# Conditioning sums moved from TensorE to GpSimd, norms by blocks of tokens, and rotary angles made earlier, in a two-part transformer kernel

## The chip, the cores and the metric

The kernel runs on one core of one Trainium2 chip. Times are device microseconds of that core for one launch. In the texts PE is TensorE, DVE is VectorE, ACT is ScalarE, POOL is GpSimd and SP is SyncE, which only issues DMAs here. The first run of numbers below is the median of three runs; the rows are of one profiled execution.

## The reference

256 tokens of 1024 features pass through two parts. The first has two layers. Each makes six vectors of 1024 (shift, scale and gate for the mixer, and again for the feed-forward) from one conditioning vector:

```
cond = silu(c)
for l in range(2):
    mod = cond @ w_ada[l] + b_ada[l]                  # 1024 x 6144
    sh1, sc1, g1, sh2, sc2, g2 = split(mod, 6)
    h = rms_norm(x, g_norm_mix[l]) * (1 + sc1) + sh1
    z = h @ w_in[l]                                   # 1024 x 2884
    mix = concat(dsa_mixer(z), hgrn2_mixer(z), gmlp_mixer(z)) @ w_out[l]
    x = x + g1 * mix
    h = rms_norm(x, g_norm_ffn[l]) * (1 + sc2) + sh2
    y = swiglu(h) if l == 0 else moe_swiglu(h)        # 8 experts, top 2
    x = x + g2 * y
x = rms_norm(x, g_final)
```

The second part (a forgetting attention, two feed-forwards with a short convolution, and a sparse attention) has no conditioning. It has a rotary embedding of its own with other angles (`positions_2`), needed for the tokens and for 15 compressed keys. All arithmetic is fp32.

## The kernel before

**Weights.** All large weights pass through one ring. SP loads slots of 1 MB (128 partitions x 2048 values) into `raw`, six places deep, in a fixed order of names: ada00, in0, out0, ada01, ffn0, ada10, in1, out1, ada11, the experts, then the second part. ACT copies a slot to `w_hi` (L792, rounded to the short matmul type, four places), DVE subtracts to make `w_lo` (L1631, in the place of `raw`), and PE multiplies three times per tile (`three`, L1127 to L1129: high by high, high by low, low by high). `w_used` counts slots that PE is done with; SP's load of slot n waits for slot n−6. An ada stage is one of four: `ada{l}0` makes shift, scale and gate ahead of the mixer, `ada{l}1` those ahead of the feed-forward, each in 12 slots and six groups of 512 columns.

**An ada stage.** DVE and ACT spread the conditioning vector over 128 columns, as high and low part (L973, L1739), in the place of the activations' columns `xT`. PE multiplies it with the slots, so that each of the 128 rows of the result is the same. DVE adds each group into `arena[:, 0:3*D]`, where POOL's queue had loaded the bias (L723), spread over all partitions. `mod[:, 0]` is the shift, `mod[:, 1]` the scale, `mod[:, 2]` the gate. The stage waits for the gate's last use (`mod_free`), and the columns `xT` of the layer before it are done with.

**A norm.** `x_ready` is signalled by DVE after X is written. ACT squares X in two blocks of 128 tokens (L869) with a sum, DVE and ACT make the reciprocal root (L874), DVE scales both blocks into H (L1655) and adds the shift (L1646). One signal `rows_ready`; then PE transposes 16 tiles of 128x128 (L1166) bank by bank of PSUM, and ACT and DVE copy each bank out as high (L862) and low (L1678) part. PE goes on when all four banks are out.

**A mixer.** Behind `in{l}` DVE applies rope (L1776 and L1646: four products and two sums a time, four times), picks the top 64 keys by eight rounds of maxima and replacements, and runs an attention with PE and ACT; then come the recurrence in eight levels, the group gating and `out{l}`, whose results DVE multiplies with the gate and adds to X.

**POOL.** It only issues small loads, in the order of the code: constants, x, c, positions, router, biases, norm gains, per layer the small tables, the lower-bound rows of layer 1 (behind `lb_free`), the spatial weights (behind `ws_free`). A gain is loaded into one place, behind `gain_free`.

**The second embedding.** After the last layer of the first part DVE waits for the small loads, the second positions among them, and makes the angles for both blocks and the compressed keys (`angles`, L1760 to L1767); ACT takes the sines; then the next norm begins.

Of the kernel before, what the change touches and what calls it, by code (L numbers as in the profile page):

```python
# [31 lines left out]
P = 128  # L32
# [152 lines left out]
def build(nc, a, consts, out):  # L185

    with ExitStack() as ctx:
# [32 lines left out]
        mod_free = semaphore("mod_free")  # L220
# [92 lines left out]
        ld_first = semaphore("ld_first")  # L313
        ld_const = semaphore("ld_const")
# [68 lines left out]
        posf = sm(3)  # L383
        tick = sm(2)
        posi = small[:, sm.at:sm.at + 3].bitcast(I32)
        sm.at += 3
# [45 lines left out]
        h_LF = Cut(arena)(768, b=2)  # L432
# [167 lines left out]
        ORDER = ["ada00", "in0", "out0", "ada01", "ffn0", "ada10", "in1", "out1", "ada11", "over", "moe",  # L600
# [25 lines left out]

        @block.sync
        def _(sp):
# [4 lines left out]
            def load(src, nk, nf):  # L633
                nonlocal n
                r = n % RAW
                if n >= RAW:

                    sp.wait_ge(w_used, n - RAW + 1)
                dst = raw[:, r, 0:nk * nf].rearrange("p (k f) -> p k f", k=nk)
                sp.dma_start(dst, src).then_inc(raw_full[r], 16)  # L640
                n += 1

# [27 lines left out]
            for name in ORDER:  # L670
# [5 lines left out]
                elif name == "over":  # L676
# [4 lines left out]
                    with sp.Else():  # L681

                        for r, sem in enumerate(raw_full):
                            total = 16 * ((ROUTED - 1 - r) // RAW + 1)
# [9 lines left out]
            assert n == len(LEN)  # L694
# [7 lines left out]
        def _(pool):  # L702
# [3 lines left out]
            def load(dst, src, sem, **how):  # L706
# [6 lines left out]
                 allow_slow_non_contiguous=True)  # L713
            load(router, a["moe_w_router"][0].rearrange("(c p) e -> p c e", p=P), ld_first)
# [5 lines left out]
            def ada_bias(l, half):  # L720
                if (l, half) != (0, 0):
                    pool.wait_ge(mod_free, got(mod_free))
                load(arena[:, 0:3 * D], a["b_ada"][l, half * 3 * D:(half + 1) * 3 * D].partition_broadcast(P),  # L723
                     ld_mod)

            for l in range(2):
                ada_bias(l, 0)
# [8 lines left out]
                load(vn_b, a["gmlp_vnorm_b"][l].partition_broadcast(P), ld_lp)  # L736
                if l:
# [6 lines left out]
                ada_bias(l, 1)  # L744
                gain_row(a["g_norm_ffn"][l])
            gain_row(a["g_final"])
# [3 lines left out]
            for dst, name in ((ksg, "ks_gain_2"), (kwg, "kw_gain_2"), (kcg, "kc_gain_2")):  # L750
# [3 lines left out]
            load(posi[:, 0:2], a["positions_2"][0].rearrange("(b p) -> p b", p=P), ld_lp,  # L754
                 allow_slow_non_contiguous=True)

# [355 lines left out]
        def _(pe):  # L1112
# [136 lines left out]
            def dense():  # L1249
# [23 lines left out]
                for g in range(N_GROUPS):  # L1273
                    for m in range(2):
                        hidden(g, m)
                    if g:
                        down(g - 1)
# [1162 lines left out]
```

## Time and profile before

| | us |
|---|---|
| median of 3 runs | 2801.14 (2799.39 to 2801.37) |
| the profiled execution's own time | 2796.36 |
| its span, first to last instruction | 2794.5 |
| PE busy | 2369.7 (85%) |
| DVE busy | 1970.1 (70%) |
| ACT busy | 1407.1 (50%) |
| POOL busy | 28.0 (1%) |

The busy time of PE comes from modelled ends of pipelined products and is no measure of PE at its peak. Times inside the run are counted from the span's start. The mean granted clock of PE is 0.902 of its full one. The mean DMA rate is 211 GB/s over the span.

### The profile page before, as it was taken

The page shows a single profiled execution, that of the slowest core. Times are in us where ns is not written, and L with a number is a line of the kernel's source. Part 1 is how long each engine was busy: PE and PEld are TensorE (multiplying, and loading weights), DVE is VectorE, ACT ScalarE, POOL GpSimd, SP SyncE. Part 2 cuts the span into 40 slices and gives each one's busy share as a digit, 9 for nine tenths or more (in the row PEclk, how much of TensorE's full clock was granted, in tenths as well). Part 3 has the DMA queues.
Part 4 walks back from the last instruction along what each step waited for, and adds up shares of the span by engine and source line. Part 5 has one row for each costly group of instructions (what it writes and reads, how often), then busy time and mean ns, then how long its engine had stood idle before and what let it go on. Part 6 is the DMA issues. An engine that isn't in the chain of part 4 may idle for free.

```text
span 2794.5 us, 31076 instructions
## 1 busy us (share of the span) xinstructions
PE 2369.7 (85%) x12719; PEld 2011.4 (72%) x12719; DVE 1970.1 (70%) x2343; ACT 1407.1 (50%) x1356; POOL 28.0 (1%) x52
## 2 busy tenths in 40 slices
PE   4936799886477799999999999997658899778898
PEld 4726699765366688888888888886546898656898
DVE  6565754476456688888888888887554788675787
ACT  5322443342423477777767777776324443355432
POOL 0000000000000000000000000000000000000000
PEclk9957899988578799999999999999878999878999
DMA  9400745663014699999999999998321455321453
GB/s 344 140 30 5 271 155 192 202 223 110 6 34 151 251 354 357 354 356 354 357 341 348 359 354 356 355 356 303 102 90 48 142 189 191 109 76 53 148 186 106
DMA packets 293718, 590.71 MB, mean 211 GB/s; under 512 B 11702, under 2 KB 86564, under 8 KB 292928
## 3 DMA queue, kind: packets, MB, share of 16 engines
q1 hardware_dynamic: 289872, 572.33, 58.1%
q0 software_dynamic: 3696, 16.32, 1.9%
q8 instruction: 102, 1.67, 0.2%
q14 instruction: 48, 0.39, 0.0%
HBM read 587.56 MB, written 1.05 MB: 211 GB/s over the span
## 4 chain that ended last, share of the span: by engine, by line
PE 59%; DVE 4%; ACT 2%; DMA 1%; issue 1%; POOL 0%; SPq 0%; DVEq 0%; ACTq 0%
PE ps L1127 18%; PE ps L1129 17%; PE ps L1128 17%; PE ps L1209 1%; PE ps L1333 1%; PE ps L1316 1%; PE ps L1294 1%; PE ps L1194 1%; ACT arena L892 1%; DVE arena L1793 1%; PE ps L1232 1%; DVE arena L1646 1%; PE ps L1166 1%; PE ps L1183 0%; DVE w_lo L1631 0%
## 5 line engine op out<-in xcount | busy, mean ns | idle before, releaser
L792 ACT ACTIVATE w_hi<-raw 128x2048 fp32r<-128x2048 f32 x548 | 1041.7, 1907 | 593.8 <-PE ps L1129 462.6
L1631 DVE TENSOR_TENSOR w_lo<-raw,w_hi 128x2048 fp32r<-128x2048 f32 x548 | 1225.2, 2273 | 56.7 <-ACT w_hi L792 41.1
L1127 PE MATMUL ps<-w_hi,xT_hi 128*128 128x512 f32 (+3 forms) x1600 | 637.1, 398 | 46.3 <-DVE xT_lo L1739 24.7
L1129 PE MATMUL ps<-w_hi,xT_lo 128*128 128x512 f32 (+3 forms) x1600 | 623.5, 390 | 0.0
L1128 PE MATMUL ps<-w_lo,xT_hi 128*128 128x512 f32 (+3 forms) x1600 | 623.0, 389 | 0.0
L1127 PEld LDWEIGHTS ps<-w_hi,xT_hi 128*128 128x128 f32 x1600 | 307.1, 192 | 113.6 <-DVE xT_lo L1739 26.1
L1128 PEld LDWEIGHTS ps<-w_lo,xT_hi 128*128 128x128 f32 x1600 | 307.4, 192 | 61.8 <-issue 3.4
L1129 PEld LDWEIGHTS ps<-w_hi,xT_lo 128*128 128x128 f32 x1600 | 306.4, 191 | 62.3
L1127 PE MATMUL ps<-xT_hi,w_hi 128*128 128x256 f32 x1056 | 299.8, 284 | 4.3 <-DVE xT_lo L1678 4.3
L1129 PE MATMUL ps<-xT_hi,w_lo 128*128 128x256 f32 x1056 | 299.5, 284 | 0.0
L1128 PE MATMUL ps<-xT_lo,w_hi 128*128 128x256 f32 x1056 | 299.5, 284 | 0.0
L1127 PE MATMUL ps<-w_hi,aT_hi 128*128 128x512 f32 (+1 forms) x744 | 287.9, 387 | 1.4 <-DVE aT_lo L1897 1.4
L1128 PE MATMUL ps<-w_lo,aT_hi 128*128 128x512 f32 (+1 forms) x744 | 287.4, 386 | 0.0
L1129 PE MATMUL ps<-w_hi,aT_lo 128*128 128x512 f32 (+1 forms) x744 | 287.0, 386 | 0.0
L1127 PEld LDWEIGHTS ps<-xT_hi,w_hi 128*128 128x128 f32 x1056 | 203.4, 193 | 6.2 <-DVE xT_lo L1678 5.1
L1128 PEld LDWEIGHTS ps<-xT_lo,w_hi 128*128 128x128 f32 x1056 | 203.3, 193 | 1.1
L1129 PEld LDWEIGHTS ps<-xT_hi,w_lo 128*128 128x128 f32 x1056 | 203.3, 193 | 0.0
L1127 PEld LDWEIGHTS ps<-w_hi,aT_hi 128*128 128x128 f32 (+1 forms) x744 | 137.8, 185 | 29.9 <-DVE aT_lo L1897 1.6
L1129 PEld LDWEIGHTS ps<-w_hi,aT_lo 128*128 128x128 f32 (+1 forms) x744 | 137.6, 185 | 28.7
L1128 PEld LDWEIGHTS ps<-w_lo,aT_hi 128*128 128x128 f32 (+1 forms) x744 | 137.7, 185 | 27.1
L1166 PE MATMUL ps<-const,Z 128*128 128x128 f32 x144 | 30.5, 400 | 107.4 <-DVE small L1752 107.4
L956 ACT ACTIVATE aT_hi<-arena 128x512 fp32r<-128x512 f32 x33 | 20.9, 632 | 172.2 <-DVE arena L1878 172.2
(322 smaller groups left out, 1946.0 us busy)
## 6 DMA issues: line engine op xcount, KB each, us to landing
raw<-in_moe_w_gate SPq DMA_DIRECT2D x112, 1024.0 KB, 5.6
raw<-in_moe_w_up SPq DMA_DIRECT2D x112, 1024.0 KB, 5.3
raw<-in_moe_w_down SPq DMA_DIRECT2D x112, 1024.0 KB, 5.4
raw<-in_w_ada SPq DMA_DIRECT2D x48, 1024.0 KB, 5.2
raw<-in_f_w_up SPq DMA_DIRECT2D x44, 1024.0 KB, 5.1
raw<-in_f_w_down SPq DMA_DIRECT2D x22, 1024.0 KB, 5.0
raw<-in_w_in SPq DMA_DIRECT2D x20, 1024.0 KB, 5.8
raw<-in_a_w_in SPq DMA_DIRECT2D x12, 1024.0 KB, 5.3
```

What stands on the lines that cost most here:

```text
L792: act.activation(w_hi[:, k % HI, 0:LEN[k]], raw[:, r, 0:LEN[k]], ACT.Copy).then_inc(w_hi_ready, 1)
L892: last = act.activation(x, x, ACT.Exp, bias=negmax[:, s % 4, h:h + 1], accum_out=rowsum[:, s % 4, h:h + 1])
L1127: pe.matmul(out_, lh, rh, start=start, stop=False)
L1128: pe.matmul(out_, lh, rl, start=False, stop=False)
L1129: return pe.matmul(out_, ll, rh, start=False, stop=stop)
L1166: last = pe.transpose(ps[:, bank + k, (c % 2) * T + b * P:(c % 2) * T + (b + 1) * P], src[:, b, c * P:(c + 1) * P], ident)
L1194: last = pe.transpose(ps[0:kw, 6 + u // 4, (u % 4) * P:(u % 4 + 1) * P], bufs[at.nth[i] % 3][:, x:x + kw], ident)
L1209: last = pe.matmul(ps[:, 4 * (1 - s % 2) + h % 2, (h // 2) * 256:(h // 2) * 256 + W], q(h), k(h), start=True, stop=True)
L1232: last = pe.matmul(out_[:, j * P:j * P + w], v[0 if shared else 2 * j + parity](c), Ts[s % 2][0:kw, x:x + w], start=at.first[i] and c == 0 ...
L1294: last = pe.transpose(ps[:, 2, j * P:(j + 1) * P], e_act[:, j * P:(j + 1) * P], ident)
L1316: last = pe.matmul(ps[:, 6 + c // 4, c % 4 * P:(c % 4 + 1) * P], H[:, b, c * P:(c + 1) * P], pick[:, b, :], start=b == 0, stop=b == 1)
L1631: dve.tensor_tensor(w_lo[:, k % RAW, 0:LEN[k]], raw[:, k % RAW, 0:LEN[k]], w_hi[:, k % HI, 0:LEN[k]].bitcast(F32), ALU.subtract).then_inc( ...
```

## The change

Five things change.

1. Only shift and scale of layer 0's mixer (`ada00`, now 8 slots) stay on PE in the old way. The other 40 slots go through the same ring `raw`, but POOL consumes them: it multiplies a slot in place by the conditioning vector (one scalar per partition and row block), adds the four row blocks together, and adds the result to the part in `arena`, which it first sets to zero, with the bias in row 0. The result is a partial sum in each partition. PE then sums over the partitions by a product with a matrix of ones (`conditioned`), and ACT copies it back from PSUM.
2. The ring has slots of two owners. `AFTER` says behind which slot of PE a slot of POOL is loaded: gate{l}0 behind every second slot of in{l}; shift{l}1 (eight slots) all behind the last slot of in{l}; gate01 and shift10 (the shift and scale of layer 1's mixer) behind every second slot of ffn0; gate11 behind out1's last slot. SP issues in that order and waits for the owner of the place.
3. Norms by blocks: `x_ready` and `rows_ready` are signalled once per block of 128 tokens, and PE transposes the first block's eight tiles when this block is ready.
4. The second positions are loaded at the start, and their angles are made by DVE behind the third group of ada00.
5. The recurrence's `h_LF` moves from `arena` to `mix`, since `arena[:, 0:3*D]` now holds sums during the mixer.

```diff
-                for half in range(2):
-                    s[f"ada{l}{half}"] = linear_slots(a["w_ada"][l, :, half * 3 * D:(half + 1) * 3 * D], 3 * D)
+                if l == 0:
+                    s["ada00"] = linear_slots(a["w_ada"][0, :, 0:2 * D], 2 * D)
...
+        for l in range(2):
+            k = BASE[f"in{l}"]
+            part(f"gate{l}0", l, 0, True, range(k + 1, k + 9, 2))
+            part(f"shift{l}1", l, 1, False, [k + 11] * 8)
+            if l == 0:
+                k = BASE["ffn0"]
+                part("gate01", 0, 1, True, range(k + 1, k + 9, 2))
+                part("shift10", 1, 0, False, range(k + 9, k + 25, 2))
+            else:
+                part("gate11", 1, 1, True, [BASE["out1"] + 3] * 4)
...
+            def weighted_sums(name, l, half, at, width, free=None):
+
+                if free is not None:
+                    pool.wait_ge(free, got(free))
+                dst = arena[:, at:at + width]
+                c0 = half * 3 * D + at
+                step(pool.memset(dst, 0.0))
+                load(dst[0:1, :], a["b_ada"][l:l + 1, c0:c0 + width], ld_bias)
+                pool.wait_ge(ld_bias, got(ld_bias, 16))
+                first, count = PARTS[name]
+                for i in range(count):
+                    n = RING_POOL[first + i]
+                    sem, total = filled(n)
+                    pool.wait_ge(sem, total)
+                    w = raw[:, n % RAW, :].rearrange("p (k f) -> p k f", k=4)
+                    o = dst[:, i // 2 * FG:i // 2 * FG + FG]
+                    c = condT[:, i % 2 * 4:i % 2 * 4 + 4]
+                    step(pool.tensor_tensor(w, w, c.unsqueeze(2).to_broadcast([P, 4, FG]), ALU.mult))
+                    step(pool.tensor_tensor(w[:, 0:2, :], w[:, 0:2, :], w[:, 2:4, :], ALU.add))
+                    step(pool.tensor_tensor(o, o, w[:, 0, :], ALU.add))
+                    ins = pool.tensor_tensor(o, o, w[:, 1, :], ALU.add)
+                    ins.then_inc(ada_used, 1)
+                    pool.wait_ge(ada_used, sent(ada_used))
...
+            def conditioned(name, at, banks):
+
+                first, count = PARTS[name]
+                pe.wait_ge(ada_used, first + count)
+                pe.wait_ge(ada_rows, got(ada_rows, 0))
+                for i, bank in enumerate(banks):
+                    pe.matmul(ps[:, bank, :], ones, arena[:, at + i * FG:at + i * FG + FG],
+                              start=True, stop=True).then_inc(ada_out, 1)
+                got(ada_rows, len(banks))
...
-                to_columns(mix, 3)
+                to_columns(mix, 3, blocks=False)
+                conditioned(f"gate{l}0", 2 * D, (4, 5))
                 linear(f"out{l}")
-                pe.wait_ge(cond_cols, got(cond_cols))
-                linear(f"ada{l}1", 1, True)
+                conditioned(f"shift{l}1", 0, (6, 7, 4, 5))
                 to_columns(H)
                 if l == 0:
-                    dense()
+                    dense(lambda: conditioned("gate01", 2 * D, (2, 3)))
+                    conditioned("shift10", 0, (0, 1, 2, 3))
```

ACT's copies stand in its queue at the same places, ahead of the norm's squares. POOL's queue has gate{l}0 and shift{l}1 ahead of the lower-bound rows and the spatial weights, and gate{l}1 (with shift10 in layer 0) ahead of the next gain.

## Rows read from the trace of the kernel before

**Rows 1.** The page's chain that ended last, shares by engine.
```profile
PE 59%; DVE 4%; ACT 2%; DMA 1%; issue 1%; POOL 0%; SPq 0%; DVEq 0%; ACTq 0%
```

**Rows 2.** Stretches: length, busy per engine (instructions), PE clock, DMA share, GB/s.
```profile
24.50:62.60 38.10, 34.44 (x144) 28.07 (x144) 33.42 (x21) 24.94 (x13) 0.00 (x0) 0.99 1.04 385
...
78.30:142.00 63.70, 63.70 (x288) 53.56 (x288) 32.15 (x22) 20.86 (x12) 0.00 (x0) 0.97 0.49 164
142.00:272.50 130.50, 65.30 (x476) 55.93 (x475) 76.83 (x206) 35.38 (x65) 1.27 (x2) 0.64 0.04 13
...
354.00:541.00 187.00, 186.98 (x1320) 176.11 (x1320) 88.56 (x55) 74.74 (x56) 0.00 (x0) 1.00 0.55 180
...
546.20:585.00 38.80, 35.00 (x144) 28.45 (x144) 32.60 (x23) 23.97 (x13) 2.64 (x5) 0.91 0.98 351
...
600.50:665.00 64.50, 63.76 (x288) 53.58 (x288) 32.83 (x24) 20.89 (x12) 0.00 (x0) 0.97 0.51 166
...
941.00:1940.00 999.00, 995.26 (x4552) 816.97 (x4552) 854.77 (x516) 716.84 (x480) 0.00 (x0) 1.00 0.97 354
```

**Rows 3.** DVE in order of time, in and behind ada00: start, length.
```profile
44.07 0.68 DVE L1746 TENSOR_TENSOR arena<-arena,ps 128x512 f32<-128x512 f32 x1
...
62.58 0.15 DVE L1752 COPY small<-small 128x1 f32<-128x1 f32 x1
```

**Rows 4.** DVE in order of time, between the two parts.
```profile
1959.60 0.15 DVE L1752 COPY small<-small 128x1 f32<-128x1 f32 x1
1963.31 0.17 DVE L2221 CAST small<-small 128x2 f32<-128x2 int32 x1 [3.56 <-DMA small<-in_positions]
...
1969.25 0.34 DVE L1752 COPY small<-small 128x1 f32<-128x1 f32 x2
1972.23 0.17 DVE L1652 TENSOR_SCALAR small<-small 128x2 f32<-128x2 f32 x1 [2.64 <-ACT Z L869]
```

**Rows 5.** DVE's groups by shape, 541 to 600 us: busy, mean ns of one.
```profile
L1631 DVE TENSOR_TENSOR w_lo<-raw,w_hi 128x2048 fp32r<-128x2048 f32 x12 | 27.0, 2288 | 4.1 <-DMA arena<-in_b_ada 4.0
...
L1678 DVE TENSOR_TENSOR xT_lo<-ps,xT_hi 128x512 fp32r<-128x512 f32 x4 | 2.8, 691 | 2.3 <-ACT xT_hi L862 2.2
...
L1646 DVE TENSOR_TENSOR Z<-Z,arena 128x1024 f32<-128x1024 f32 x2 | 2.4, 1224 | 0.1
```

**Rows 6.** DVE in order of time, behind out0 and behind ada01.
```profile
299.64 0.53 DVE L1752 COPY small<-small 128x1 f32<-128x1 f32 x3
...
339.31 0.15 DVE L1752 COPY small<-small 128x1 f32<-128x1 f32 x1
```

**Rows 7.** The same behind ffn0 and ada10, and behind out1 and ada11.
```profile
546.06 0.53 DVE L1752 COPY small<-small 128x1 f32<-128x1 f32 x3
...
584.81 0.15 DVE L1752 COPY small<-small 128x1 f32<-128x1 f32 x1
...
846.59 0.53 DVE L1752 COPY small<-small 128x1 f32<-128x1 f32 x3
...
885.37 0.15 DVE L1752 COPY small<-small 128x1 f32<-128x1 f32 x1
```

**Rows 8.** PE in order of time, experts' end: two fp32 products as four records.
```profile
1940.10 1.96 PE L1333 MATMUL ps<-arena 128*128 128x512 f32 x4 [1.21 <-ACT arena L833]
```

**Rows 9.** DMA issues, 1951 to 1982 us: KB each, us to landing.
```profile
Z<-in_a_norm POOLq DMA_DIRECT2D x1, 512.0 KB, 4.3
```

**Rows 10.** A piece of the chain that ended last: start, length.
```profile
1976.60 3.66 PE ps L1166 x16
```

**Rows 11.** The norm's squares on ACT: durations ns least, median, most.
```profile
L869 ACT ACTIVATE Z<-X x18: 1038/1040/1056, 62.8 to 2589.3; 128x1024 f32<-128x1024 f32 x18
```

**Rows 12.** POOL in order of time: a memset, and layer 1's lower-bound rows.
```profile
0.28 0.10 POOL L2428 MEMSET const-float32-1.0<- 128x1 f32 x1
...
720.91 0.54 POOL L707 DMA_DIRECT2D arena<-in_hgrn_lb_logits  x1 [171.77 <-DVE small L1752]
```

**Rows 13.** DVE in order of time: rope's first four products.
```profile
143.15 1.29 DVE L1776 TENSOR_TENSOR arena<-Z,small 128x224 f32<-128x224 f32 x4
```

More of the change, by code:

```diff
@@ L598, in build @@
         N_GROUPS = F_DENSE // DG
-        ORDER = ["ada00", "in0", "out0", "ada01", "ffn0", "ada10", "in1", "out1", "ada11", "over", "moe",
+        ORDER = ["ada00", "in0", "out0", "ffn0", "in1", "out1", "over", "moe",
                  "fa_in", "fa_out", "conv0", "kv", "nsa_in", "kc", "vc", "nsa_out", "conv1"]
@@ L625, in build, with part, filled @@
         ROUTED = BASE["over"]
+        AFTER, PARTS = {}, {}
+        pool_slots = []
+        def part(name, l, half, gate, after):
+            c0 = half * 3 * D + (2 * D if gate else 0)
+            slots = linear_slots(a["w_ada"][l, :, c0:c0 + (D if gate else 2 * D)], D if gate else 2 * D)
+            PARTS[name] = len(pool_slots), len(slots)
+            for slot_, k in zip(slots, after):
+                AFTER.setdefault(k, []).append(len(pool_slots))
+                pool_slots.append(slot_)
+        for l in range(2):
[8 more added lines that the diff above has]
+                part("gate11", 1, 1, True, [BASE["out1"] + 3] * 4)
+        RING, RING_POOL, OWNER = [], [], []
+        for k in range(len(LEN)):
+            RING.append(len(OWNER))
+            OWNER.append((w_used, k + 1))
+            for j in AFTER.get(k, ()):
+                RING_POOL.append(len(OWNER))
+                OWNER.append((ada_used, j + 1))
+        def filled(n):
+            return raw_full[n % RAW], 16 * (n // RAW + 1)
         @block.sync
@@ L641, in load @@
                 n += 1
+            k = 0
+            def load(src, nk, nf):
+                nonlocal k
+                fill(src, nk, nf)
+                for j in AFTER.get(k, ()):
+                    nk, nf, src = pool_slots[j]
+                    fill(src, nk, nf)
+                k += 1
             def dense(wg, wu, wd):
@@ L969, in _, with second_sines @@
             rotary_sines()
+            def second_sines():
+                act.wait_ge(angles_ready, got(angles_ready))
+                for s in (sin2, cos2):
+                    act.activation(s, s, ACT.Sin).then_inc(sines, 1)
+                for s in (sinc, cosc):
+                    act.activation(s[0:N_CMP, :], s[0:N_CMP, :], ACT.Sin).then_inc(sines, 1)
             def cond_columns():
@@ L1747, in evac, with second_angles @@
                     dve.wait_ge(lin_evac, sent(lin_evac))
-                linear(name, evac)
+                def second_angles():
+                    dve.wait_ge(ld_late, 32)
+                    step(dve.tensor_copy(posf[:, 2:4], posi[:, 2:4]))
+                    step(dve.tensor_copy(posf[0:N_CMP, 4:5], posi[0:N_CMP, 4:5]))
+                    inv2 = const[:, C_INV2:C_INV2 + 8]
+                    for b in range(TB):
+                        angles(posf[:, 2 + b:3 + b], inv2, 8, sin2[:, b, :], cos2[:, b, :])
+                    angles(posf[0:N_CMP, 4:5], inv2[0:N_CMP, :], 8, sinc[0:N_CMP, :], cosc[0:N_CMP, :])
+                    beat().then_inc(angles_ready, 1)
+                    dve.wait_ge(angles_ready, sent(angles_ready))
+                linear(name, evac, {2: second_angles} if name == "ada00" else {})
             def beat():
```

210 lines of the change are left out of this document (118 added, 92 removed).

## Prediction

> **What bounds the kernel now.** I read the page's busy shares and its chain first: TensorE (PE) carries 59% of the chain that ended last [rows 1]. That is a mean over unlike stages, so I cut the trace by stage. The reader is to see three kinds. In the experts everything runs at the DMA's pace, 354 GB/s at a share of 0.97 [rows 2]; nothing in the change touches those 1000 us. In the in-projections and dense layers PE is busy end to end (63.7 of 63.7 us, 187.0 of 187.0) while VectorE (DVE) is half busy and the DMA engines too [rows 2]. Between them lie the mixers: 130 us with PE at 65 and DVE at 77 [rows 2], a chain of DVE, ScalarE (ACT) and PE steps where each waits for the other, so that a longer DVE step is a longer run. The four conditioning stages (twelve slots each) are of a fourth kind: the one of 546 to 585 us has PE at 35.0, DVE at 32.6 and DMA at 351 GB/s [rows 2], all for one vector. Nothing is beside them: X is final when they begin and the norm waits at their end.
>
> **The change part by part.** PE keeps the first eight slots of 48. The other forty go to GpSimd (POOL). Times below are in the profiled execution (2796.36 us; its span is 2794.5, and the median of the runs is 4.8 us over it).
>
> *Start.* PE does 4 groups of columns instead of 6. The third one's sum starts at 44.07 and takes 0.68 [rows 3], to 44.75. Behind it the new hook makes the second embedding's angles on DVE, which took from 1963.31 to 1969.25 at their old place [rows 4]: 5.9 us. Then two splits of 2.29 [rows 5] and the last sum of 0.7: x is released at about 56.1, where it was at 62.6 [rows 3]. Gain 6.5. If the DMA's pace hid the angles it would be 12; DVE has 0.2 us free per slot here, so I don't count on it. The two position loads issued ahead of the router's put at most 1.2 us before the first product, but the stream of slots paces this stage (385 GB/s [rows 2]); I take nothing.
>
> *The stages behind out0, ffn0 and out1.* What goes is the time from the last write of X to the beat that released it: 299.64 to 339.46, 39.8 us [rows 6]; 546.06 to 584.96 and 846.59 to 885.52, 38.9 each [rows 7]. In their place:
> - Four products with ones and four ACT copies ahead of the norm's squares. They are plain fp32 products over 512 columns; two such (four records) take 1.96 us [rows 8], so four take 3.9 and a copy 0.7. Behind out0 and out1 PE is done 2.9 us ahead of X's last write (four DVE steps of 0.7), so squares start 1.7 us late. Behind ffn0 DVE needs 5 us for X anyway, which hides it all, and squares of the first block run under the second block's add: 1.0 gained.
> - Two products for the gate ahead of out0, out1 and of ffn0's last down: 2.0 each. Before the experts' last down they fall into PE's wait for the activations' low part; I take 0.4.
> - The gain of layer 1's first norm. Its load waits for the add that ends ffn0 and used to be hidden by the stage that goes. A gain takes 4.3 us to land [rows 9], the squares 2.4, and the wait stands ahead of the root: 3.3 with the issue. This is what is late next at that place. The gains of the other two norms are loaded early.
> - The norm by blocks: PE's sixteen transposes take 3.66 us after DVE's last row [rows 10]. Now eight run under DVE's second block, and the last eight hand over a bank every 0.46 instead of 0.92. Four copies and four subtractions then set the pace: 1.05 gained per norm.
>
> Sums: out0 −39.8+1.7+2.0−1.05 = −37.2; ffn0 −38.9−1.0+2.0+3.3−1.05 = −35.6; out1 −38.9+1.7+2.0−1.05 = −36.2. Together −109.0.
>
> *Angles at their old place.* The norm before the second part begins at 1972.23; X was scaled at 1959.60 [rows 4]. Afterwards it waits for its own gain: issued at about 1960.1, landed 4.3 later, 1964.4. Gain 7.8, and 1.05 for blocks: −8.9.
>
> *Other norms.* Three of them, 1.05 each, and in two the first block's squares (1.04 each [rows 11]) go under X's second write: −5.2.
>
> *POOL's queue.* The sums stand in it before other loads. Layer 1's lower-bound rows are loaded behind shift11; DVE asked for them at 720.9 [rows 12], 120 us after in1's start at 600.5 [rows 2]. By the price below POOL is free at 46 + 8×9.8 = 124, so 3 or 4 late; I add 3. The spatial weights and the final gain are asked for later.
>
> Sum without any hold-up between POOL and DVE: −6.5−1.05−109.0−8.9−5.2+0.4+3 = −127, or 2674 on the median.
>
> *POOL's price.* Per slot it multiplies 128x2048, adds 128x1024 and twice 128x512. No row shows POOL computing; it has only one-column memsets at 0.1 us and DMA issues [rows 12]. Below, the nearest rows are DVE's for the same shapes: 2.29+1.22+0.69+0.69 = 4.9 us a slot [rows 5]. Above I go to three times that, 14.7. I take twice, 9.8, an estimate of mine between these. The Trainium skill (page GPSIMD Engine Reference, section 3.1) gives 4497 ns for POOL's two-input add at 2048 fp32, which would make a slot 9.2; no row here shows it. At 9.8 POOL keeps pace with the ring. In ffn0 one POOL slot stands behind two of PE, and 187/33×2 = 11.3 us pass per pair [rows 2]. With two slots of slack in the ring, 12×(T−11.3) may reach 22.6, so T up to 13.2 costs nothing. gate11 (39 us) ends as the experts' first loads are issued, 40 us behind out1's end in the new order.
>
> *What POOL does to DVE.* This decides the size, and no row shows it. POOL's sums of shift01 and shift11 lie in the mixers. Their slots load once in0's eighth is used, 46 us after its start; in0 ends at 63.7 [rows 2], so 6.2 of 8 slots, 25 POOL instructions, run beside DVE where DVE sets the pace. gate11's 16 run beside the norm and the router, and some 3 each beside the norms of ffn0 and in1. That is 72 instructions of 2.45 us mean. Low end: they don't disturb DVE, 0. High end: every DVE step with two SBUF tensors waits for one POOL instruction until these are used up: 25×2.45 = 61 in each mixer (rope alone has 24 such steps, of which a row shows the first four [rows 13]), 13 steps in norm and router make 32, the two norms 15: 169. My value: POOL's running instruction holds DVE up once per burst of such steps, for what is left of it. Lengths 4.6, 2.5, 1.4, 1.4 leave 1.6 on the mean. Bursts: eleven per mixer (rope, four in the index, four scalings, two in the log-sigmoid), ten in norm and router, one for each of the two norms: 34×1.6 = 54. I choose it near the low end because much of the mixer is not of this kind: the 32 maxima and replacements read one tensor, the score steps read PSUM. The splits in in0 and ffn0 are held up too but DVE is idle for half of these stages.
>
> **Forecast:** 2801 − 127 + 54 = 2728.
>
> **The rivals.**
> - *POOL and DVE don't hold each other up.* For it: nothing in the trace forbids it. Then 2674.
> - *They alternate, the other side.* If POOL's next instruction gets in between each two DVE steps, rope's 1.3 us for four products [rows 13] becomes 1.3 plus four POOL instructions. All of it costs 169: 2801−127+169 = 2843, slower. It decides from 127 us, three quarters of its reach; at half, 85, the time is 2759. For it: each DVE step here waits for its own end before the next starts, which leaves POOL a gap. Against it: POOL has such gaps too, and DVE's products of rope are issued four at a time. The Trainium skill (page SBUF — State Buffer, section Who interferes with whom) says that a DVE instruction with two SBUF inputs contends with a POOL instruction that reads SBUF, and the later one is blocked fully. By that rule a hold-up is certain and only its count open; no row here has POOL computing, so the trace neither agrees nor differs.
> - *POOL too slow for the ring.* At 14.7 a slot: ffn0 loses 12×3.4−22.6 = 18, the experts' first loads (slots behind gate11) 19, the lower-bound rows come at 46+118 = 164 instead of 120, 44, of which 3 are in the sum. Together 78: 2752.
> - *The norms' overlap brings nothing,* since ACT's and DVE's columns set the pace already: 8 us less gain than forecast, 2736. Inside the range.
>
> **How the numbers follow.** Forecast 0.40 (2705 to 2750 as its own range), no hold-up 0.27, alternation in part 0.16 (2750 to 2795), alternation in full 0.08, slow POOL 0.06, the rest 0.03. The range runs from a little under the first rival, 2660, to 2795, which leaves full alternation out. A measurement here tells 0.2%, about 5.6 us, from no change. Slower than that only in full alternation and part of the rest, 0.09; within it 0.03; faster 0.88.
>
> **What would show it.** PE should run 480 fewer weight products and 20 plain fp32 ones in their place; x released near 56 us; no PE gap with stages of 39 us behind out0, ffn0, out1; POOL busy for forty times some 10 us. For the hold-up: DVE's steps of rope, 0.32 us each now, with a maximum of several us, or idle time before them without a semaphore; layer 0's mixer longer than 130.5 us. In0's and ffn0's stages should stay at 64 and 187 us. The prediction falls if ffn0 is longer, if the experts' first load is late, or if POOL's slot is above 13 us.

## The result and the profile after

| | before | after |
|---|---|---|
| median of four runs | 2801.26 us (2799.39 to 2802.87) | 2856.78 us (2852.72 to 2860.22) |
| ratio, 95% interval | | 1.0203 (1.0188 to 1.0217) |
| span of the profiled execution | 2794.5 | 2858.4 |
| mean granted clock | 0.902 | 0.874 |

The change makes the kernel 2.0% slower. The prediction was 2728, in a range of 2660 to 2795, with 0.88 on faster. The page of the kernel after, in its busy times, its tenths and its chain:

```profile
PE 2290.3 (80%) x12279; PEld 1940.3 (68%) x12279; DVE 2003.9 (70%) x2263; ACT 1333.3 (47%) x1331; POOL 462.4 (16%) x223
...
POOL 3490048737600500000000000000000000000000
PEclk8856789988567599999999999999777999868999
...
PE 57%; DVE 5%; ACT 2%; DMA 1%; issue 1%; DVEq 0%; POOL 0%; SPq 0%; ACTq 0%; POOLq 0%
```

PE lost 79 us of work against before, as planned, and the span grew by 64. The chain [rows 1] hardly changed its shares, so it doesn't tell where the time went. I cut the trace at one instant that every stage has: the end of the last `xT_lo` (activations' columns ready). The lengths between these, in us:

| from columns ready to columns ready | before | after |
|---|---|---|
| start to in0 | 78.2 | 83.3 |
| in0 to out0 (in0, rope, index, attention, recurrence) | 194.3 | 258.3 |
| out0 to ffn0 (out0, [stage], norm) | 81.4 | 52.6 |
| ffn0 to in1 (ffn0, add, [stage], norm) | 246.6 | 236.6 |
| in1 to out1 | 219.7 | 276.3 |
| out1 to the router | 79.8 | 53.2 |
| router to the next part's first (router, experts, angles) | 1081.6 | 1078.3 |
| second part | 812.9 | 819.8 |

The conditioning stages (in brackets) are gone: 29 and 27 us less behind the two outs. The two stretches from in to out, which the prediction left as they were but for the hold-up, grew by 64 and 57. DVE in layer 0, in order of time (start, length, how many merged, and the idle time before with what ended it):

```profile
172.38 2.68 DVE L1753 TENSOR_TENSOR w_lo<-raw,w_hi 128x2048 fp32r<-128x2048 f32 x1 [30.39 <-ACT w_hi L883]
183.10 2.67 DVE L1753 TENSOR_TENSOR w_lo<-raw,w_hi 128x2048 fp32r<-128x2048 f32 x1 [8.04 <-ACT w_hi L883]
185.69 0.48 DVE L1842 COPY Z<-ps 128x324 f32<-128x324 f32 x1
...
186.74 7.94 DVE L1919 TENSOR_TENSOR arena<-Z,small 128x224 f32<-128x224 f32 x4
194.71 5.04 DVE L1768 TENSOR_TENSOR Z<-arena 128x224 f32<-128x224 f32 x2
199.79 8.70 DVE L1919 TENSOR_TENSOR arena<-Z,small 128x160 f32<-128x160 f32 x4
208.52 3.72 DVE L1768 TENSOR_TENSOR Z<-arena 128x160 f32<-128x160 f32 x2
212.28 2.28 DVE L1919 TENSOR_TENSOR arena<-Z,small 128x224 f32<-128x224 f32 x4
214.59 0.82 DVE L1768 TENSOR_TENSOR Z<-arena 128x224 f32<-128x224 f32 x2
```

There are two losses, one behind the other. PE is done with in0 at 147.6, but DVE takes its last columns out at 185.7: ahead of that copy it stands in line with two splits of **out0's** weights, for which ACT waits 39 us. Then rope's products take 7.9 us where they took 1.3 [rows 13], up to 213, and from there they have their old length. ACT's wait:

```profile
170.37 1.91 ACT L883 ACTIVATE w_hi<-raw 128x2048 fp32r<-128x2048 f32 x1 [39.33 <-DMA raw<-in_w_out]
181.16 1.91 ACT L883 ACTIVATE w_hi<-raw 128x2048 fp32r<-128x2048 f32 x1 [8.88 <-DMA raw<-in_w_out]
```

and POOL at the same time:

```profile
164.21 1.26 POOL L812 TENSOR_TENSOR arena<-arena,raw 128x512 f32<-128x512 f32 x1
165.55 3.60 POOL L809 TENSOR_TENSOR raw<-raw,small 128x2048 f32<-128x2048 f32 x1
169.23 2.35 POOL L810 TENSOR_TENSOR raw<-raw 128x1024 f32<-128x1024 f32 x1
171.65 1.26 POOL L811 TENSOR_TENSOR arena<-arena,raw 128x512 f32<-128x512 f32 x1
172.99 3.19 POOL L812 TENSOR_TENSOR arena<-arena,raw 128x512 f32<-128x512 f32 x1
...
212.14 1.26 POOL L812 TENSOR_TENSOR arena<-arena,raw 128x512 f32<-128x512 f32 x1
```

A slot takes POOL 8.7 us when DVE has no long step beside it (3.60, 2.34, 1.26, 1.26 and the gaps); beside DVE's splits it takes 10.8 to 14.9 in ffn0, 12.6 on the mean of the ten slots there. `in{l}`'s loop on DVE splits two slots ahead of the one it takes out, so at its end it wants out0's first two. These stand in the ring behind shift01's eight slots. With six places, they can be loaded only when shift01's third and fourth slots are summed: at about 165 and 176. The last row shows rope's slow steps end when POOL is done, at 213.4.

There are three more places, by DVE's rows beside POOL: the angles in the start run from 43.02 to 61.53, 18.5 us instead of 5.9; the four scalings of the norm behind out0 take 3.24, 2.17, 2.18 and 4.51, each 1.2 to 1.3 before; and ffn0 takes 208 us instead of 187, its splits 3226 ns each instead of 2288 [rows 5]. In ffn0 this is 30 us without and 30 us with a stall (columns: stretch, its length, busy of PE, PEld, DVE, ACT, POOL, granted clock, DMA share, GB/s):

```profile
420.00:450.00 30.00, 30.00 (x210) 28.16 (x209) 18.68 (x9) 12.59 (x10) 23.72 (x11) 1.00 0.83 284
480.00:510.00 30.00, 22.37 (x144) 21.01 (x143) 21.62 (x7) 9.61 (x7) 29.22 (x11) 0.86 0.82 280
```

POOL is busy for 29.2 of 30 us in the second. The idle PE then costs twice: its granted clock is 0.86 over the second stretch, where it was 1.00 in all of ffn0 before [rows 2].

### The profile page after: what moved, and what is told of

Its sections match the earlier page's. It is cut to its first block, busy times and chain, and to the rows that moved or that the text cites. A ratio compares the mean times of both kernels' runs of the same rounds, so it can differ in the third digit from the quotient of the medians.

```text
span 2858.4 us, 30246 instructions
## 1 busy us (share of the span) xinstructions
PE 2290.3 (80%) x12279; PEld 1940.3 (68%) x12279; DVE 2003.9 (70%) x2263; ACT 1333.3 (47%) x1331; POOL 462.4 (16%) x223
## 3 DMA queue, kind: packets, MB, share of 16 engines
HBM read 582.36 MB, written 1.05 MB: 204 GB/s over the span
## 4 chain that ended last, share of the span: by engine, by line
PE 57%; DVE 5%; ACT 2%; DMA 1%; issue 1%; DVEq 0%; POOL 0%; SPq 0%; ACTq 0%; POOLq 0%
PE ps L1230 17%; PE ps L1232 17%; PE ps L1231 17%; PE ps L1314 1%; PE ps L1450 1%; PE ps L1299 1%; PE ps L1433 1%; PE ps L1411 1%; DVE arena L1936 1%; ACT arena L985 1%; DVE w_lo L1753 1%; PE ps L1337 1%; DVE arena L1768 1%; DVE xT_lo L1800 0%; PE ps L1270 0%
## 5 line engine op out<-in xcount | busy, mean ns | idle before, releaser
L1753 DVE TENSOR_TENSOR w_lo<-raw,w_hi 128x2048 fp32r<-128x2048 f32 x508 | 1182.1, 2362 | 153.6 <-ACT w_hi L883 142.4
L883 ACT ACTIVATE w_hi<-raw 128x2048 fp32r<-128x2048 f32 x508 | 965.0, 1906 | 681.7 <-PE ps L1232 268.2
L1230 PE MATMUL ps<-w_hi,xT_hi 128*128 128x512 f32 (+4 forms) x1440 | 574.9, 399 | 28.1 <-DVE xT_lo L1800 10.6
L1232 PE MATMUL ps<-w_hi,xT_lo 128*128 128x512 f32 (+4 forms) x1440 | 561.0, 390 | 0.0
L1231 PE MATMUL ps<-w_lo,xT_hi 128*128 128x512 f32 (+4 forms) x1440 | 560.3, 389 | 0.0
L1230 PEld LDWEIGHTS ps<-w_hi,xT_hi 128*128 128x128 f32 x1440 | 277.5, 193 | 88.2 <-DVE xT_lo L1800 12.4
L1231 PEld LDWEIGHTS ps<-w_lo,xT_hi 128*128 128x128 f32 x1440 | 277.5, 193 | 56.0 <-issue 4.1
L1232 PEld LDWEIGHTS ps<-w_hi,xT_lo 128*128 128x128 f32 x1440 | 276.7, 192 | 55.4
L1230 PEld LDWEIGHTS ps<-xT_hi,w_hi 128*128 128x128 f32 x1056 | 208.1, 197 | 19.5 <-DVE w_lo L1753 11.3
L809 POOL TENSOR_TENSOR raw<-raw,small 128x2048 f32<-128x2048 f32 x40 | 156.5, 3912 | 117.7 <-DMA raw<-in_w_ada 95.9
```

Source lines behind the costliest of these rows:

```text
L809: step(pool.tensor_tensor(w, w, c.unsqueeze(2).to_broadcast([P, 4, FG]), ALU.mult))
L883: act.activation(w_hi[:, k % HI, 0:LEN[k]], raw[:, r, 0:LEN[k]], ACT.Copy).then_inc(w_hi_ready, 1)
L1230: pe.matmul(out_, lh, rh, start=start, stop=False)
L1231: pe.matmul(out_, lh, rl, start=False, stop=False)
L1232: return pe.matmul(out_, ll, rh, start=False, stop=stop)
L1753: dve.tensor_tensor(w_lo[:, r, 0:LEN[k]], raw[:, r, 0:LEN[k]], w_hi[:, k % HI, 0:LEN[k]].bitcast(F32), ALU.subtract).then_inc(w_lo_ready, 1)
```

## The experiments

Line numbers in the rows are those of each kernel's own file. The kernel before ran beside each group at 2797 to 2799.

**1. No early splits.** `in{l}`'s loops on ACT and DVE stop at in's own last slot; out's splits are made when `out{l}` begins.

```diff
-upto(BASE[name] + len(SL[name]) - 1 + HI - 1)
+upto(BASE[name] + len(SL[name]) - 1 + (0 if name in ("in0", "in1") else HI - 1))
```

> The splits of out0's and out1's weights are no longer made ahead of the end of in0 and in1, but at the start of out0 and out1. Theory A (two losses: 38.6 us a layer because those early splits wait for slots that stand in the ring behind GpSimd's eight, and a hold-up in which each VectorE step with two SBUF inputs waits for one GpSimd instruction): the 38.6 goes, but rope now starts while six more of GpSimd's slots are to come, so its 24 steps wait for some 24 GpSimd instructions, 53 us instead of 32; out0 and out1 start some 5 us later for their first split. Net gain about 14 a layer: 2829 (2815 to 2845). Rival B (the ring is the only loss, the slow rope is a consequence of it): all 38.6 come back less 5, 2790. Rival C (the wait was for something else): no change or 5 a layer slower, 2857 to 2867.

Measured: 2846.9, 1.0182 (1.0145 to 1.0219). Ten us gained where I had said 28, and just outside my range. in0's last columns are out at 149.6 instead of 186.7, as they should, and then:

```profile
149.60 8.08 DVE L1920 TENSOR_TENSOR arena<-Z,small 128x224 f32<-128x224 f32 x4
157.71 6.12 DVE L1768 TENSOR_TENSOR Z<-arena 128x224 f32<-128x224 f32 x2
...
190.37 8.70 DVE L1920 TENSOR_TENSOR arena<-Z,small 128x160 f32<-128x160 f32 x4
199.10 2.64 DVE L1768 TENSOR_TENSOR Z<-arena 128x160 f32<-128x160 f32 x2
201.78 6.03 DVE L2150 COPY arena<-Z 128x256 f32<-128x256 f32 x2
```

POOL beside the first four of these products:

```profile
148.65 3.60 POOL L809 TENSOR_TENSOR raw<-raw,small 128x2048 f32<-128x2048 f32 x1
152.33 2.37 POOL L810 TENSOR_TENSOR raw<-raw 128x1024 f32<-128x1024 f32 x1
154.77 1.29 POOL L811 TENSOR_TENSOR arena<-arena,raw 128x512 f32<-128x512 f32 x1
156.14 1.29 POOL L812 TENSOR_TENSOR arena<-arena,raw 128x512 f32<-128x512 f32 x1
```

Rope takes 52.1 us for its 24 steps; POOL starts 24 instructions in that time, one for each of DVE's, and a slot takes it 8.7 to 8.8 us, no longer than without rope beside it. So the two losses hide one another: what the ring gives back, the hold-up takes, since POOL ends at 210.3 where it ended at 213.4. Late splits of out cost 8 us a layer (out0 to ffn0 60.7 instead of 52.6). Rival B falls.

**2 and 3. The time of POOL without its arithmetic.** In shift01 and shift11 POOL passes each slot's time with small loads (2), or with fills that write and don't read (3); these sums are left out.

```diff
-step(pool.tensor_tensor(w, w, ..., ALU.mult))   # and three adds
...
+for _ in range((2, 1, 2, 2, 1, 2, 2, 1)[i]):    # run 2
+    load(dst[0:1, :], a["b_ada"][...], ld_bias); pool.wait_ge(ld_bias, ...)
...
+for _ in range(4):                              # run 3, and one fill of half the size
+    step(pool.memset(w, 0.0))
```

> In shift01 and shift11 GpSimd does no arithmetic: each slot is given back after one or two small loads that it waits for, about 8.9 us a slot as before; these sums are left out. Theory A: the early splits of out0 and out1 still wait (about 38 us a layer, since the slots come back as late), while rope is back at 9.8 us: 45 us less, 2812. Rival B (the stall at the end of in0 is VectorE held up by GpSimd's arithmetic, not the ring): the stall goes as well, 2735. Rival C (the small loads take GpSimd longer or shorter than 8.9 a slot): 4 slots times the difference a layer.

> As the one before, but GpSimd passes the time of each slot of shift01 and shift11 with four fills of 128x2048 (1.81 us each in the profile) and one of 128x1024, which write SBUF and read nothing; these sums are left out. Theory A, with a hold-up that needs GpSimd to read: as the run with small loads, 2812. Rival (any GpSimd instruction on SBUF holds VectorE up): rope stays at 32 us or more and the time near 2857.

Measured: 2790.7 (0.9973, 0.9960 to 0.9985) and 2815.4 (1.0058, 1.0041 to 1.0075). With small loads rope's first four products take 1.30 us again, and in0's last copy still waits, until 176.1: the stall is the ring's, not the arithmetic's. By the fourth slot the loads were some 10 us ahead of POOL's sums (in0's last copy at 176.1 instead of 185.7), in each layer, which is the 20 that this run came out below 2812. Run 3 says what is held up:

```profile
184.09 1.30 DVE L1924 TENSOR_TENSOR arena<-Z,small 128x224 f32<-128x224 f32 x4
...
192.02 2.63 DVE L2154 COPY arena<-Z 128x256 f32<-128x256 f32 x2
194.69 1.73 DVE L2155 TENSOR_SCALAR small<-Z 128x8 f32<-128x8 f32 x1
```

Beside POOL's fills (1.81 us each) the steps with two SBUF inputs run at full speed, but the copies take 1.3 each and the small scaling 1.73 instead of 0.17. So two kinds of hold-up come apart: DVE's steps with a second SBUF input wait for POOL's instructions that read (7.94 us for rope's four products beside the sums, 1.30 beside the fills), and its copies and scalings from SBUF to SBUF wait for those that only write, too. The Trainium skill (page SBUF — State Buffer, section Who interferes with whom) says just that: two SBUF inputs contend with a GpSimd instruction that reads and not with one that only writes, while `copy` and `tensor_scalar` can enter a two-port mode that contends with GpSimd. This trace agrees on both counts, by the 1.30 us of rope's four products and the 1.3 us of a copy.

**4. No sums at all.** POOL gives each of its forty slots back after a one-column fill; all its sums are left out.

> GpSimd gives each of its forty slots back after a one-column fill; all its sums are left out, the loads, waits, products with ones and the norms by blocks stay. Theory A: every loss that comes from GpSimd's time goes: 2857 less 77 (ring), 45 (rope), 27 (norms), 19 (ffn0), 12 (angles in the start) and 4 (gate copies): about 2673, the prediction's own sum without a hold-up. Rival (the gains themselves were smaller than worked out, for instance the blocks of the norm): 2685 to 2700.

Measured: 2713.4 (0.9690, 0.9674 to 0.9706), 40 above the sum that I had. So even without POOL's time something is lost. PE waited 60.3 us in two waits for heads, 30 each, where it waited 9.9 each before. DVE's first step after 21 us of idle time at the end of in0, a split of out0's weights, and then the last two of POOL's eight slots:

```profile
148.47 2.29 DVE L1750 TENSOR_TENSOR w_lo<-raw,w_hi 128x2048 fp32r<-128x2048 f32 x1 [21.06 <-ACT w_hi L880]
```

```profile
141.13 0.10 POOL L809 MEMSET raw<- 128x1 f32 x1 [2.61 <-DMA raw<-in_w_ada]
143.85 0.10 POOL L809 MEMSET raw<- 128x1 f32 x1 [2.62 <-DMA raw<-in_w_ada]
```

The eight slots come one every 2.7 to 4.1 us, and out0's first lands behind them at 146.5, 13.4 us after PE is done with in0. The early split waits for eight loads even if nobody computes.

**5. The other half alone.** The kernel before, with norms by blocks and the second angles in the start; all conditioning on PE.

```diff
-beat().then_inc(rows_ready, 1)
...
+last.then_inc(rows_ready, 1)        # in the loop over the two blocks
```

> The kernel before with one half of the change: norms, squares and transposes by blocks, and the second embedding's angles behind the third column group of the first stage. All six conditioning stages stay on TensorE, with nothing on GpSimd. By the prediction's terms: between the parts 8.9 less, two first blocks' squares and eight norms by blocks 2.1 and 8.4 less, the angles' 5.9 more in the start: 13 less, 2785 if the kernel before is at 2798. Rival (the angles at the start are hidden by the pace of the loads): 19 less. Rival (the blocks bring nothing, ScalarE's and VectorE's columns set the pace): 4 less.

Measured: 2794.9, 0.9992 (0.9981 to 1.0002). No change, where my terms gave 13 less. In the trace (2789.2 long) 9.2 us went between the parts, from the experts' last products to columns ready, as said, and the five stretches from in0 to the router are 5.5 shorter together; but the second part became 5.5 longer (818.4 for 812.9), where the terms had some 5 less. The first 4 us of six stages that follow a norm, before (in0, ffn0, in1, and three of the second part):

```profile
78.30:82.30 4.00, 4.00 (x10) 3.13 (x11) 4.00 (x2) 1.01 (x1) 0.00 (x0) 0.50 0.00 0
353.90:357.90 4.00, 3.95 (x33) 3.95 (x34) 4.00 (x2) 1.06 (x1) 0.00 (x0) 1.00 0.00 0
600.50:604.50 4.00, 3.97 (x9) 3.14 (x10) 4.00 (x2) 1.05 (x1) 0.00 (x0) 0.50 0.00 0
1981.60:1985.60 4.00, 3.94 (x17) 3.29 (x18) 4.00 (x3) 1.08 (x1) 0.00 (x0) 1.00 0.00 0
2181.60:2185.60 4.00, 3.95 (x20) 3.95 (x21) 2.19 (x1) 1.07 (x1) 0.00 (x0) 0.57 0.00 0
2599.80:2603.80 4.00, 3.93 (x32) 3.93 (x33) 2.21 (x2) 1.09 (x1) 0.00 (x0) 1.00 0.02 4
```

and two of the same with norms by blocks:

```profile
354.20:358.20 4.00, 3.99 (x23) 4.00 (x24) 4.00 (x2) 0.63 (x1) 0.00 (x0) 0.64 0.00 0
...
1970.80:1974.80 4.00, 3.96 (x11) 3.10 (x12) 4.00 (x2) 0.66 (x1) 0.00 (x0) 0.60 0.00 0
```

Three of the six stages began at a granted clock of 1.00 before; in run 5 none does (0.50 to 0.64), and PE gets 23 products done in the time of 33, and 11 in that of 17. Four us at 0.60 to 0.64 instead of 1.00 (a part of them at the lower level, 1.2 GHz) are 1.5 us of work lost, more than the 1.05 that a norm was to gain. PE ahead of the second part's first stage, its first product before, then its transposes and first product in run 5:

```profile
1981.66 0.50 PE L1127 MATMUL ps<-w_hi,xT_hi 128*128 128x512 f32 x1 [1.41 <-DVE xT_lo L1678]
```

```profile
1965.19 3.38 PE L1166 MATMUL ps<-const,Z 128*128 128x128 f32 x16 [21.48 <-DVE Z L1705]
1970.84 0.50 PE L1126 MATMUL ps<-w_hi,xT_hi 128*128 128x512 f32 x1 [2.27 <-DVE xT_lo L1679]
```

By blocks no bank is complete before the last eight transposes, so the copies end later behind them: in all six stages PE waits 2.0 to 2.3 us between its last transpose and the first product, where it waited 1.4. In the layers' norms the transposes also stand in two pieces, 0.6 us apart; in the second part they still run in one. That the longer wait lowers the clock fits these rows but wasn't tried by itself, and it doesn't always do so: run 8 below, with the same norms and waits of 2.0, has two stages of the second part that begin at 1.00, and its second part takes 812.7. Two such starts are 3 of the 11 us or so by which the second part of run 5 missed its terms. From its first columns to those behind its attention it is 2.4 longer (134.8 for 132.4), 1.5 of them in these first four us; the rest is open.

**6 and 7. The sums in the mixer on PE, and POOL kept off the norms.** Run 6 lets PE sum shift01's and shift11's slots, with plain fp32 products of one column of the condition and the raw slot: four slots behind in, while DVE does rope, four behind the first attention scores, while DVE does the index. No early splits. Run 7 also has POOL wait, ahead of each part, for the end of the norm beside it.

```diff
+pe.matmul(ps[row:row + 1, bank, :], condT[:, c:c + 1], raw[:, n_ % RAW, ...], start=c == 0, stop=c == 7)
+pool.wait_ge(shift_free, 2 * l + 1)     # run 7, ahead of gate{l}0; 2 * l + 2 ahead of gate{l}1
```

> The changed kernel with the eight slots of shift01 and of shift11 summed by TensorE instead of GpSimd: plain fp32 products of one column of the condition with the raw slot (four per slot), four slots behind in0 while VectorE does rope, four behind the first attention scores while VectorE does the index; the splits of out's weights wait for out as in the run without early splits. Theory A (ring wait 38.6 and hold-up of rope 22.5 a layer both come from GpSimd's eight slots there): 122 go, TensorE's own sums cost some 11 a layer (16 us for four slots beside 10 us of rope, later splits of out): 2757 (2745 to 2775). Rival B (the clock falls while TensorE waits for slots, and a product takes 1.7 instead of 0.85 us): another 15 a layer, 2787. Rival C (the ring still holds out's slots back so long that out0 starts late): above 2800.

> As the one before, and GpSimd starts each of its parts only when the norm ahead of it has signalled its end, so that none of its instructions runs beside the first stage's angles or the three norms behind out0, ffn0 and out1. Theory A: the angles fall from 18.5 to 5.9 us and the norms to their old length (12, 10, 7 and 10 us): 35 less than the run before, less what the later sums lose in in0, ffn0 and the router (some 5 to 10): about 28 less, 2729. Rival (a hold-up is only put off: the same number of GpSimd's instructions meets VectorE's steps elsewhere): no difference.

Measured: 2755.5 (0.9842, 0.9828 to 0.9856) and 2725.4 (0.9730, 0.9715 to 0.9746). Both as theory A said, within 4 us. Taking POOL's 16 slots out of the mixers is worth 101 us (91 against run 1, which has no early splits either); moving its first instructions from beside the norms and the angles another 30, net of 13 that are lost from the router on (1088.5 for 1075.1 in run 6). In run 7 the start is 69.9 us to columns ready (83.3 after, 78.2 before), so the 6.5 and the block's 1.05 that the prediction gave it are there once POOL is away. The rival "only put off" falls: it depends on what DVE does at that time.

**8. POOL's sums behind rope.** As run 1, with a wait for rope's end ahead of the eight slots.

```diff
+pool.wait_ge(heads_ready, int(name[5]) + 1)
```

> The run without early splits, with GpSimd waiting for the end of rope ahead of its eight slots of shift01 and shift11. There rope's 24 steps took 52 us. Theory A1 (held up are steps whose inputs are all in SBUF and copies, but not the 32 maxima and replacements): rope is back at 5 us, and the index's 16 two-input steps and small scalings meet GpSimd instead, 35 us: gain some 20 a layer, 2807. Theory A2 (maxima and replacements are held up too): the index stretches until GpSimd is done, 2847 or more. Rival (hold-up happens only when a step arrives in the middle of a burst of GpSimd, once): 2760.

Measured: 2815.4 (1.0061, 1.0046 to 1.0075). Rope is back at 8 us, and the index beside POOL looks like this:

```profile
166.33 7.47 DVE L1779 SCALAR_TENSOR_TENSOR arena<-arena,small 128x128 f32<-128x128 f32 x3
173.83 4.99 DVE L1770 TENSOR_TENSOR arena<-arena,const 128x128 f32<-128x128 f32 x2
178.85 0.29 DVE L2175 MAX8 small<-arena 128x8 f32<-128x128 f32 x1
...
179.26 0.27 DVE L2176 MATCH_REPLACE8 arena<-small,arena 128x128 f32<-128x128 f32 x1
```

Three steps with two SBUF inputs take 7.5 us instead of 1.1; the maxima and replacements keep their length, and so do DVE's steps that read PSUM (12 copies of 128x512 out of PSUM beside POOL's sums took 0.69 each, as elsewhere). A1 holds, though 8 us above the 2807 that it had said.

**9 and 10. The rest of ffn0, and more on PE.** Run 9 is run 7 with POOL's twelve slots spread over the whole of ffn0. In run 10 PE also sums gate01 and gate11 while the norm behind out runs on ACT and DVE; POOL keeps gate00, gate10 and shift10, spread; and the first splits of out and ffn0 come where ACT and DVE are idle.

```diff
+part("gate01", 0, 1, True, range(k + 1, k + 11, 3))     # run 9
+part("shift10", 1, 0, False, (k + 13, k + 15, k + 18, k + 20, k + 23, k + 25, k + 27, k + 29))
...
+part("shift10", 1, 0, False, range(k + 1, k + 30, 4))   # run 10, from here on
...
+row_sums(f"gate{l}1", 0, 4)             # PE, behind conditioned(f"shift{l}1", ...)
...
+upto(BASE[f"out{l}"] + 1)               # ACT, ahead of the last root of the mixer
```

> The calm run (2725), with GpSimd's twelve slots of ffn0 spread over the whole stage (ring places k+1 to k+29 in place of k+1 to k+23). Ffn0 is 21 us longer than before there, and GpSimd busy 29.3 of 30 us in its middle. Theory A (crowding: VectorE's splits are held up one behind the other until TensorE waits, and the ring waits for GpSimd): half of the 21 comes back, 2715. Rival B (each slot costs its share wherever it stands): no difference, 2725. Rival C (the last sums are late for the stage's end): slower, 2735.

> TensorE also sums gate01 and gate11 (four slots each) with plain fp32 products, behind out0's and out1's last product, while the norm runs on ScalarE and VectorE; GpSimd keeps gate00, gate10 and shift10, the last spread over ffn0; the first splits of out and ffn0 are made a little ahead, where ScalarE and VectorE are idle. Theory A: against the calm run's 2725, 14 less between out1 and the experts (their first loads no longer wait for GpSimd), some 14 less in ffn0 (eight slots of GpSimd instead of twelve), 3 less for each earlier split, and 2 more each where TensorE's 14 us of sums end behind the norm's 12: 2690 (2675 to 2710). Rival (TensorE's sums wait for their slots, whose loads begin only when out's slots are used, and delay the norm's transposes by some 8 us each): 2705 or more. Rival (VectorE's splits in ffn0 lose the same with eight slots): 2704.

Measured: 2709.2 (0.9671, 0.9650 to 0.9692) and 2689.2 (0.9603, 0.9587 to 0.9619). Ffn0 in run 7, in run 9 and in run 10:

```profile
316.00:524.00 208.00, 196.19 (x1327) 183.26 (x1328) 129.12 (x56) 76.12 (x58) 149.93 (x50) 0.96 0.67 223
```

```profile
316.00:508.00 192.00, 191.10 (x1325) 179.22 (x1326) 135.20 (x56) 76.02 (x58) 150.71 (x50) 0.99 0.72 241
```

```profile
316.00:507.00 191.00, 190.99 (x1327) 179.02 (x1328) 113.26 (x57) 78.33 (x59) 88.39 (x32) 0.99 0.67 221
```

POOL's busy time is the same in runs 7 and 9 and DVE's no shorter, and 15 us of stage go (213 for 228 from columns to columns), more than the half of 21 that theory A had said: it was where the slots stood, not how many. Run 10 is 4% under the kernel before and, by the two ratios, 5.9% under the changed one. Its 24 slots take PE 3.5 us each (four in 13.89 us, at a granted clock of 1.00), nearly all inside waits that were there: from in0's columns to out0's it takes 197.2 us, 194.3 before.

**11. Shorter instructions.** Run 1 with each slot cut into eight POOL instructions over 512 columns instead of four.

> The run without early splits (2847), with each of GpSimd's slots cut into eight instructions over 512 columns (about 1.1 us each) in place of four (3.6, 2.3, 1.3, 1.3). Same sums, same slots. Theory A (a VectorE step waits for exactly one GpSimd instruction, whatever its length): rope's 24 steps take 24 x 1.2 = 29 us instead of 52; the rest of GpSimd's work meets the index (16 steps, 18 us); norms and ffn0 lose half of what they lost: about 2817. Rival B (VectorE waits until GpSimd has done a slot's worth of bytes, or the two share the time): rope stays at 50 us and more, 2847 or slower. Rival C (more instructions give GpSimd's overhead only): 2855.

Measured: 2808.8 (1.0032, 1.0022 to 1.0043). Two of rope's groups:

```profile
160.54 4.81 DVE L1923 TENSOR_TENSOR arena<-Z,small 128x224 f32<-128x224 f32 x4
165.38 2.70 DVE L1771 TENSOR_TENSOR Z<-arena 128x224 f32<-128x224 f32 x2
```

Rope takes some 30 us instead of 52: 1.2 per step. One DVE step waits for one POOL instruction, and what it costs is that instruction's length: 1.1 us for a piece of the multiply instead of 3.6 for the whole. The same sums in twice as many pieces are 38 us faster.

**12. The prediction's own sum.** Run 4 (all of POOL's sums left out) without early splits, and with out's first splits placed as in run 10.

> The run without GpSimd's sums (2713), and in it no split of out's weights ahead of in's end; the first of out0's and out1's are split late in the mixer instead, where ScalarE and VectorE wait for TensorE. Without sums TensorE still stood still for 30 us behind in0 and in1, where it was 9.9 before. Theory A (the eight loads themselves, in order in the ring ahead of out's, hold the early splits up for 20 us even if GpSimd takes no time): 40 less and some 2 more for the moved splits, 2675, which is the prediction's sum without a hold-up (2674). Rival (the 20 us have another cause, the norm or the loads of in0): 2713 or a little more.

Measured: 2682.0 (0.9578, 0.9554 to 0.9602). PE's two waits for heads are 10.0 each again. Theory A holds: 31 of the 40 came back. What remains is in the second part, 822.1 long where it was 812.9 before and should have lost some 5 (run 5); up to there the trace takes 1860.6, and the prediction's terms give 1859.6.

## Why the prediction was wrong

**The step that failed first: "At 9.8 POOL keeps pace with the ring", from which a stall of the ring was put at nothing.** It compared POOL's time per slot with the pace of the slots, and left out who asks for a slot early. The in-order ring puts out0's weights behind shift01's eight slots, and DVE's loop wants them *ahead of its own last result*. That is 38.6 us a layer, 77 in all: some 20 a layer for the eight loads, and the rest for four slots of POOL. PE's products of in0 stayed at 64 us, as said; it was the hand-over of their result that came late. I had listed what waits behind POOL's own queue (the lower-bound rows), not what waits behind its slots in SP's.

**The hold-up, 54 us.** The term was mis-sized, and its rule ("once per burst") wrong: DVE and POOL alternate, step by step. Without any sums the kernel is 143 faster (run 4), of which 37 are the ring's; that leaves, by difference, some 106 for the hold-up. By the rows, rope alone cost 22.5 a layer, the norms 27 together, the angles 12.6, which is 85, and ffn0 21 more. The rival "They alternate" had the mechanism, with up to 169, and 0.24 in all. That its 2843 lies near the measured time is luck: it has no stall of the ring, and its hold-up is 63 too large. POOL's remaining instructions bound the hold-up, and whatever delays DVE meanwhile makes it smaller. The rule of the Trainium skill (page SBUF — State Buffer, section Who interferes with whom), that the later of two such instructions is blocked, stood beside this rival and spoke against the change; rope's rows agree with it, 7.94 us for four products instead of 1.3.

**"I take twice, 9.8".** The price of a slot was right where DVE has only short steps (8.7 us) and on the mean of the forty (10.8), but not beside splits: DVE holds POOL up too, and ffn0's ten slots took 12.6 each, more than the 11.3 that pass per pair of PE's slots.

**The splits in in0 and ffn0, put at nothing since "DVE is idle for half of these stages".** In in0 the products kept their 64 us. Ffn0 lost 21: POOL's twelve slots stood close together, and splits that are held up one behind the other are late for PE, whose clock then falls. Spread out they cost 5 (run 9).

**Angles in the start, gain 6.5.** The place was beside POOL's first two slots, which I had counted nowhere. With the norm behind it, it became a loss of 5; without POOL there both are a gain of 8.3 (run 7), where 7.55 was said.

**Norms by blocks, 1.05 each.** In the layers the stretches got shorter as said, and the second part, where the stages behind a norm began at a lower clock, took it back (run 5). Why its clock was lower is shown only in part.

**What held.** The stages' 39.8 and 38.9 went, with the small sums for products, copies and the late gain: with POOL's time out of the way and the splits moved, the sum of 2674 was measured as 2682 (run 12, which leaves the sums out). The maxima and replacements are not held up (run 8). The angles at their old place gave 9.2 for 8.9.

The rivals: *no hold-up* is excluded by rope's rows. *POOL too slow for the ring* named the lower-bound rows as what is late in a mixer, not the ring's own stall; a part of it is in ffn0. *The norms' overlap brings nothing* comes out right for the whole kernel (run 5), but not for its reason, which would hold in the layers too.

## What to carry to other kernels

When slots of another consumer are put into an in-order ring, look first for whoever reads ahead in it: a loop that prepares slot k+2 before it hands over slot k turns every slower slot in between into a stall. Before work goes to POOL, mark for each stage which DVE steps have two SBUF inputs (or copy and scale from SBUF to SBUF): in these runs each of them waited for one POOL instruction, so POOL belongs beside PSUM reads, maxima and idle time, in short instructions and spread out. And ask the idle engine first: here PE waited in the mixers and the norms, and plain fp32 products on the raw slots cost no splits and no hold-up.

## What the runs showed that I had not expected

- A POOL instruction that only writes (a fill of 1.81 us) doesn't hold up a DVE step with two SBUF inputs, but it does a copy (1.3 us instead of 0.3) and a small scaling (1.73 instead of 0.17).
- POOL is held up in turn: its last add took 3.19 us beside a DVE split of 2.68, and 1.26 alone.
- POOL's multiply of 128x2048 by a value per partition and row of 512 took 3.60 us, its add of 128x1024 2.34: 1.6 and 1.9 times DVE's steps of the same shapes [rows 5].
- A shorter norm can be followed by a stage that starts at half the clock: three stages of six began at 1.00 before, none in run 5, two of the second part in run 8. Between last transpose and first product PE waited 1.4 us before and 2.0 to 2.3 by blocks.
- A conditioning sum as plain fp32 products with one column takes PE 3.5 us a slot (four slots in 13.89 us), without splits by ACT and DVE.
